# Experts sorted by token count, sixteen small ones taken four at a time in the second half of a mixture-of-experts stage

## The reference

```python
def moe_ffn(x, ...):            # 64 experts, 8 groups of 8, width 256, 8 picks a token
    scores = sigmoid(t @ w_router)
    biased = scores + router_bias
    # best 4 of 8 groups by the sum of their two best, then the best 8 experts in these
    w = scores of the 8 picks / their sum * 2.5
    h = silu(t @ w_gate[e]) * (t @ w_up[e])      # for each expert e
    routed = sum over picked e of w[e] * (h @ w_down[e])
    shared = (silu(t @ ws_gate) * (t @ ws_up)) @ ws_down
    return routed + shared
```

## Time and profile before

| | |
|---|---|
| median of 3 runs | 823.23 us (822.86 to 823.74) |
| profiled execution | 823.12 us |
| its span, first to last instruction | 821.4 us |
| PE busy | 805.8 us (98%) |
| DVE / ACT / POOL busy | 465.0 / 165.9 / 93.2 us |
| moved by DMA | 262.15 MB, mean 319 GB/s |
| gate and up, line 1478 | 1024 matmul records, about 593 ns each |
| granted TensorE clock, mean | 0.997 |

### The profile page before, as it was taken

How to read it: one execution, slowest core, us unless ns; L and a number is a source line. 1 busy time by engine, 2 the same in 40 slices (tenths; PEclk the granted TensorE clock), 3 DMA queues, 4 the chain that set the end, 5 groups by cost and what they waited for, 6 DMA issues and landing times.

```text
span 821.4 us, 11932 instructions
## 1 busy us (share of the span) xinstructions
PE 805.8 (98%) x4283; PEld 501.6 (61%) x4283; DVE 465.0 (57%) x1178; ACT 165.9 (20%) x275; POOL 93.2 (11%) x105
## 2 busy tenths in 40 slices
PE   9999999999999999999999999999999999999995
PEld 7876788888788888544545445454444445445443
DVE  6989899999841357634444334444444434334346
ACT  2210112111221004321211212112121211212126
POOL 1119800000010002100000000000000000000021
PEclk9999999999999999999999999999999999999998
DMA  8433344445489956699999999999999999999991
GB/s 329 157 128 103 117 143 150 155 149 116 141 332 418 412 180 239 215 392 418 423 425 421 423 423 425 421 427 422 422 426 424 422 427 425 421 421 420 419 380 55
DMA packets 45372, 262.15 MB, mean 319 GB/s; under 512 B 9928, under 2 KB 10696, under 8 KB 26256
## 3 DMA queue, kind: packets, MB, share of 16 engines
q1 hardware_dynamic: 40720, 252.88, 77.4%
q0 software_dynamic: 4608, 8.66, 2.8%
HBM read 267.10 MB, written 2.53 MB: 328 GB/s over the span
## 4 chain that ended last, share of the span: by engine, by line
PE 83%; DMA 9%; SPq 5%; ACT 1%; issue 1%; DVE 0%; POOL 0%; ACTq 0%; DVEq 0%; POOLq 0%
PE banks L1269 35%; PE banks L1478 21%; PE banks L1522 10%; PE banks L1441 6%; DMA high<-w_gu 5%; SPq L465 4%; DMA ring<-w_gu 3%; PE banks L1416 3%; SPq L473 2%; PE banks L1284 1%; PE banks L1296 1%; PE banks L1446 1%; PE banks L1495 1%; PE banks L1370 1%; PE banks L1302 1%
## 5 line engine op out<-in xcount | busy, mean ns | idle before, releaser
L1478 PE MATMUL banks<-high,low 128*64 128x512 f32 x848 | 230.1, 593 | 1.1 <-DMA high<-w_gu 1.0
L1269 PE MATMUL banks<-xT,ring 128*128 128x264 f32 x768 | 176.5, 390 | 0.0
L1174 DVE TENSOR_TENSOR cgb<-cgb,banks 128x264 f32<-128x264 f32 x248 | 89.8, 423 | 131.1 <-PE banks L1441 130.9
L1269 PEld LDWEIGHTS banks<-xT,ring 128*128 128x128 f32 x768 | 144.8, 191 | 30.1 <-issue 5.5
L1478 PEld LDWEIGHTS banks<-high,low 128*64 128x64 f32 x848 | 74.0, 137 | 139.4 <-issue 136.4
L1228 DVE SCALAR_TENSOR_TENSOR y_pair<-banks,sml,y_pair 128x1024 fp32r<-128x1024 f32 x31 | 39.8, 1284 | 121.9 <-ACT y_pair L729 121.9
L563 POOL DMA_INDIRECT low<-x_rows_dram,idx x32 | 31.9, 997 | 423.9 <-DVE idx L1118 402.9
L1478 PE MATMUL banks<-ring,low 128*64 128x512 f32 x176 | 77.6, 593 | 1.6 <-DMA ring<-w_gu 1.6
L1441 PEld LDWEIGHTS banks<-sw,y_pair 128*128 128x128 f32 x496 | 63.1, 188 | 25.2 <-issue 24.3
L1522 PE MATMUL banks<-high,mu 128*64 128x512 f32 x336 | 77.2, 599 | 0.0
L1441 PE MATMUL banks<-sw,y_pair 128*128 128x264 f32 x496 | 71.6, 294 | 0.2 <-DVE cgb L1174 0.2
(11 more groups left out here) (300 smaller groups left out, 860.0 us busy)
## 6 DMA issues: line engine op xcount, KB each, us to landing
high<-w_gu SPq DMA_DIRECT2D x35, 2048.0 KB, 24.4
high<-w_dn SPq DMA_DIRECT2D x40, 1024.0 KB, 22.3
ring<-w_front SPq DMA_DIRECT2D x78, 512.0 KB, 3.3
high<-w_gu SPq DMA_DIRECT2D x34, 1024.0 KB, 10.4
ring<-w_gu SPq DMA_DIRECT2D x7, 2048.0 KB, 29.0
us<-w_dn SPq DMA_DIRECT2D x11, 1024.0 KB, 22.4
ring<-w_gu SPq DMA_DIRECT2D x8, 1024.0 KB, 12.2
bgb<-w_dn SPq DMA_DIRECT2D x6, 1024.0 KB, 22.1
```

The source lines that it names most:

```text
L1174: dve.tensor_tensor(acc[:, n], acc[:, n], psum[:, bank, 0:T], ALU.add).then_inc(added, 1)
L1269: ins = pe.matmul(psum[:, 6 + n % 2, 0:T], ring[:, n % RING, k], rhs[:, k], start=(k == 0), stop=(k == KC - 1))
L1478: ins = pe.matmul(psum[SL * j:SL * j + SL, GU_BANK, :], xg[:, k, SL * j:SL * j + SL], gu[slots[j]][:, k], start=(k == 0), stop=(k == KC - 1))
```

## The change

Everything is data that the program finds out while it runs; the weights stay where they are in DRAM.

- **Order.** Experts 0 to 7 keep their places (`FIXED`), since their weights are on the way before the routing is known. The other 56 are ranked by token count: a key per expert (count x 64 + number) is compared with all others on DVE, the ranks become a 0/1 permutation `places`, and PE sorts picks and gates with it inside visit 0: three transposes after k = 1 (`turn_gates`), four matmuls after k = 4 (`sort_gates`), nine small matmuls after the loop (`count_sorted`). The sorted order goes to a table `order`, from which SP reads the expert number of each refill.
- **Quads.** Places 8 to 29 get experts of middling count, two per step as before. From place 30 on a period of eight places holds four of the 16 least used experts, processed in one step with 32 slots each, and then four of the others in two steps of two. The steps become 1 + 12 + 14 + 1 = 28: visit 0, twelve plain ones (six written out, six in a loop that here runs once), fourteen mixed ones written out, with quads at the 3rd, 6th, 9th and 12th, and the last. Overflow (over 32 in a quad, over 64 elsewhere) sets extra turns as before.
- **Buffers.** `dn_7` goes; expert 6's down weights are loaded after visit 0. A quad uses two of the three buffer pairs, and their refills both wait for the quad. Halves are loaded for the pairs of the last two steps but one (`LATE_HALVES = 2`).
- **Rows.** A way to fetch rows by matmul (`gather_rows`, `widen`) is written but not used (`BY_PRODUCTS = 0`): all rows are gathered from DRAM. Two small DMAs load the sample rows for it all the same. The shared expert's down part moves to the quads at steps 3, 6 and 9 of the mixed ones.

The diff, cut to its core:

```diff
+        FIXED = 8
+        MIXED_FROM = 13
+        MIXED = (1, 1, 2) * 4 + (1, 1)
+        STEPS = len(MIXED)
+        BY_PRODUCTS = 0
+        LATE_HALVES = 2
+        QUADS, QUAD_FROM, QUAD_STRIDE = 4, 30, 8
-        LATE_HALVES = 3
+        SHARED_AT = {2: (0, 1, 2), 5: (3, 4, 5), 8: (6, 7)}
...
-        DOWN_PAIRS = ((4, 5), (0, 1), (2, 3), (7, 5), (0, 1), (2, 3))
+        DOWN_PAIRS = ((4, 5), (0, 1), (2, 3))
...
# SP
-                sp.wait_ge(x1_scaled, KC)
-                sp.dma_start(dn[7], w_dn[6]).then_inc(dn_in[7], 16)
...
+                def expert(place):
+                    return sp.value_load(order[0:1, bass.ds(place, 1)] if not isinstance(place, int) else order[0:1, place:place + 1], min_val=0, max_val=E - 1)
+
+                refill(0, 0, SLOT_PAIRS[0], DOWN_PAIRS[0], [6, 7], halves=True)
+                sp.wait_ge(order_ready, 1)
+                for it in range(1, 1 + PER_TURN):
+                    refill(it, it, SLOT_PAIRS[it % 3], DOWN_PAIRS[it % 3], [2 * it + 6, 2 * it + 7], halves=it < EARLY_HALVES, by_place=True)
+                    if it == 1:
+                        sp.wait_ge(weights_ready, 2)
+                        sp.wait_ge(rows_stored, 16 * TC)
+                        for g in range(2):
+                            sp.dma_start(sample_rows[32 * g:32 * g + NS], x_dram[LP:T, HC * P * g:HC * P * (g + 1)]).then_inc(rows_stored, 16)
...
+                for a, pairs in enumerate(mixed_pairs):
+                    for it in pairs:
+                        if it + 3 < PAIRS:
+                            late = PAIRS - 1 - LATE_HALVES <= it + 3 < PAIRS - 1
+                            later_refill(middle, it - PER_TURN, MIXED_FROM - PER_TURN + a, last_refill if it + 3 == PAIRS - 1 else refill, **({"halves": True} if late else {}))
...
# PE, a step: size rows for each of its 2 or 4 experts
+                    slots = [s for r in pairs for s in SLOT_PAIRS[r % 3]]
+                    downs = [s for r in pairs for s in DOWN_PAIRS[r % 3]]
+                    size = 2 * SL // len(slots)
...
+                            ins = pe.matmul(psum[size * j:size * j + size, GU_BANK, :], xg[:, k, size * j:size * j + size], gu[s][:, k],
                                             start=(k == 0), stop=(k == KC - 1))
                         if k == HC - 1:
                             ins.then_inc(gu_mid, 1)
+                        if before is None and k == 1:
+                            turn_gates()
+                        if before is None and k == 4:
+                            sort_gates()
                     ins.then_inc(gu_done, 1)
+                    if before is None:
+                        count_sorted()
```

More of the change, by code:

```diff
@@ L475, in _ @@
-                sp.wait_ge(lists_ready, 1)
[L476 to L487, removed]
@@ new lines, in _, with later_refill @@
+                sp.wait_ge(lists_ready, 1)
+                middle = sp.value_load(rounds[0:1, 1:2], min_val=PLAIN - 1, max_val=MOST - 1)
+                def later_refill(q, it, step, fill, **how):
+                    places = [(q * (2 * PER_TURN) + (2 * it + 6 + j)) % E for j in range(2)]
+                    fill(q * PER_TURN + it, q * PER_TURN + step, SLOT_PAIRS[it % 3], DOWN_PAIRS[it % 3], places, by_place=True, **how)
+                with sp.Fori(0, middle) as q:
+                    for it in range(1 + PER_TURN, 1 + 2 * PER_TURN):
+                        later_refill(q, it, it, refill)
@@ L1179, in sum_last_rows, with visit @@
                     dve.tensor_reduce(dn_sums[:, 1, j:j + 1], dn[DOWN_PAIRS[1][j]][:, 1], AX.X, ALU.add).then_inc(dn_summed[1], 1)
-                def visit(it, u, before=None, last=False):
+                def visit(it, u, before, ahead=None, wide=None, last=False):
                     if last:
@@ L1412, in select, with gather_rows, columns @@
                     ins.then_inc(selected, 1)
+                def gather_rows():
+                    def columns(k):
+                        return psum[:, 2 + k // 4, (k % 4) * P:(k % 4) * P + P]
+                    for k in range(KC):
+                        for c in range(2):
+                            pe.matmul(columns(k), xrow[c][:, k * P:k * P + P], S32[:, c], start=(k % 4 == 0 and c == 0), stop=False)
+                    for h in range(HC):
+                        for g in range(2):
+                            rows = slice(32 * g, 32 * g + NS)
+                            ins = pe.matmul(columns(HC * g + h), sample_rows[rows, h * P:h * P + P], S32[rows, 2], start=False, stop=(h == HC - 1))
+                    ins.then_inc(turned, 1)
@@ new lines, in count_sorted @@
+                def count_sorted():
+                    pe.wait_ge(sort_inputs, SORTED_PICKS)
+                    for c in range(TC + 1):
+                        for b in range(min(c + 1, TC)):
+                            rows = slice(0, tok[b])
+                            before = (tri_spread[rows] if b == 2 else tri16[:]) if b == c else ones16[rows]
+                            ins = pe.matmul(psum[:, SORT_BANKS[0], c * E:c * E + E], before, pk[rows, b], start=(b == 0), stop=(b == min(c, TC - 1)))
+                    ins.then_inc(sort_products, 1)
@@ L1490, in visit @@
                         pe.wait_ge(sw_ready, it)
+                        if isinstance(before, int) and before == 0:
+                            pe.wait_ge(lists_ready, 1)
                         combine(1 - u, before, shared)
@@ L1562, in _, with loads_of @@
-                pairs = pe.snap(turns * PER_TURN + 2)
+                def loads_of(pair):
+                    return 16 * (pair // 3 + 1)
+                visit(0, 0, [0], [16], halves=1, ahead=(4, 2), gathers=16)
+                for k in range(1, 1 + PER_TURN):
+                    visit(k, k % 2, [k], [loads_of(k)], halves=1 + k // 3, before=KC * (k - 1), ahead=(2 * k + 4, 2), gathers=16 * ((k + 1) // 2 + 1))
+                mixed = n_plain(pe)
+                with pe.Fori(1, mixed) as q:
+                    for k in range(1, 1 + PER_TURN):
+                        visit(q * PER_TURN + k, k % 2, [k], [q * 32 + 16 * (k // 3 + 1)], before=q * (PER_TURN * KC) + KC * (k - 1),
+                              ahead=((q * PER_TURN + (k + 2)) % PAIRS * 2, 2), gathers=q * 48 + 16 * ((k + 1) // 2 + 1))
```

437 lines of the change are left out of this document (302 added, 135 removed).

## The result

The kernel after takes 832.01 us (median of five, 831.26 to 833.81) against 823.40 for the kernel before beside it: a ratio of 1.0109, interval 1.0095 to 1.0123, so slower by 8.6 us. Forecast were 826.6 us, slower, in a range of 823 to 832; the direction is right, the size is not: the time lies at the range's very end, 0.01 us beyond it. The profiled execution took 832.09 us, with a span of 830.3 us, 8.9 above that of before.

A forecast was written before the change was run, and what follows sets the result against it. The prediction took the DMA weight stream, full at 423 GB/s, as the bound: 823.12 + 1.2 (stream) + 0.4 (last quad's later start) + 1.8 (cold clock) = 826.5, with 0.1 to the median 826.6 us; range 823 to 832.

The forecast's parts named there:

- What cannot pay: 365 to 781 us: 56 us of PE time saved gains nothing, as the DMA engines have no idle time.
- Rival 3: Whole kernel: PE was the bound after all, so four fewer steps pay, 767 us; chance 0.02.
- Quads and the stream: Mixed steps: a quad takes 14.45 us; queued loads (the cover, 18 us) keep the stream from running dry.
- Quads and the end: Run's end: last quad waits for pair 28's whole gate and up, slack gone, +0.4; cold clock +1.8.
- the cold clock: Last quad: PE idles some 17 us before it and starts at half clock, +1.8 us, bounds 0 and +7.
- Rival 4: Quads run two by two, 24.5 us each, end 10 us later, 836 or more; chance 0.11 with longer cold stretches.
- The sort in visit 0: Visit 0: extra PE work but no wait for DVE, delaying the next loads, +0.7 us together.
- rival 5: Visit 0: DVE's sort chain misses PE by 3 us or more, 830 us; chance 0.07.
- The rows: Before visit 0: shorter queue lets rows be stored sooner and the stream start 0 to 0.7 us earlier, taken as -0.4.
- The moved load: Stream's start: expert 6's down weights, 1.05 MB, now loaded in the stream, +2.5 us, of which 1.5 comes back.
- the thin places: Early stream, rates below 423 GB/s: 330 at 358 to 365 us, closing for -1.5; 270 at 346 to 349.
- More code: Written-out steps fetch more code than loops: doubling the code queue's 0.51 MB would be +1.2 us, taken as +0.2.

The follow-up runs named there:

- e5: Kernel after with pair 28's gate and up weights loaded by halves, so the last quad can start on half a load: 830.25 us.
- e2: Kernel after with throwaway matmuls on PE while it waits for the last quad's third and fourth gate and up buffers: 829.70 us.
- e4: Kernel before with only expert 6's down weights moved, loaded after visit 0 instead of at 323.59: 825.35 us, ratio 1.0020.
- e13: Kernel after without quads, all 18 mixed steps pairs and written out, shared expert's chunks in pairs 25 to 28: 831.24 us.
- e8: Kernel after without quads, 12 of its 18 mixed pair steps back in loops, shared expert's chunks in pairs 25 to 28: 827.74 us.
- e11: Kernel of e9 with 96 increments of an unused semaphore on GpSimd written out behind each of 30 gathers: 834.86 us.
- e9: Kernel before with the loops over turns written out on every engine, nothing else changed: 824.96 us.
- e12: Kernel before, turns still in loops, with 96 increments of an unused semaphore behind every gather of the loop: 838.43 us.
- e1: Kernel after with one line changed, a quad expert's 32 slots taking ranks in the pairs' spread order: 831.43 us, ratio 1.0094.

## Why the prediction was right or wrong

**What cannot pay: right.** Four visits fewer, the same rate of 423 GB/s, PE's time gone into waits. Rival 3 (767) is out.

**Quads and the stream: right.** No slice from 374 us to the last quad falls below 414 GB/s, and the share around the last quad is 1.00 to 1.04; the cover held.

**Quads and the end: right, the size in part by luck.** Forecast +2.2, measured 2.0 (after against e5); from the landing of pair 30's second half to the end 42.5 us, forecast 42 to 43. Its halves are less exact: the cold clock was worth 1.5 us in the quad (2.3 in e2's time, not all of it the clock's), forecast 1.8; whole loads 1.8 (e5), forecast 0.4. The two overlap, presumably as each takes away the same few microseconds ahead of the landing. From the landing at 757.24 to pair 30's gate and up done at 794.01 it is 36.8 us; the sum has 14.45 + 14.04 + 6.87 + 1.8 = 37.2. Rival 4 is out.

**The sort in visit 0: nearly right.** Visit 1's gate and up began at 358.75, 2.9 behind 355.85, of which 0.9 was the start; forecast 1 to 2. PE's extra work was some 2.3 us for 1.8, and its longest wait there 0.34, so rival 5 is out. The rows did come sooner: in an execution 0.8 late the first gather landed at 339.75 (339.63 before), and PE no longer waited for it (0.61 in the earlier trace rows). But PE's own work ahead of it had grown by as much, and its turn began at 340.56 against 339.68, the start's difference: 0 for -0.4.

**The moved load: the step that gave back too much.** I took +2.5 - 1.5 = +1.0; alone it cost 1.9 (e4). The bytes were right; filling the thin places brought 1.1 in the windows and 0.6 in the time.

**More code: the step that failed.** "Steps written out instead of looped fetch more code", doubling it "would be +1.2, I take +0.2": I priced bytes as shared by all lanes, and read one instruction queue of two. Measured, 12 steps written out or looped are 3.5 us (e13, e8), 23 more fetches on q14 alone 8.5 us of landing (e11). At 0.37 us a fetch, an estimate, the kernel after's nine are 3.3 us; how much its three further fetches on q8 add was not measured. By bytes its stream stood 3.6 to 4.1 us behind before's from 370 us on, and pair 30's second half landed 6.6 late, so some 3 us are lateness that the sum over all lanes does not show. Read as a share of 16 lanes q14 is 0.1% of the span; a load waits for the lane that the fetches hold up.

The ledger by spans: before 821.4; moved load 823.8 (e4); sort, table and looped pairs 825.5 (e8), +1.7 with four fetches more; the last quad's landing with pair 28 by halves 828.3 (e5), +2.8 with five fetches more; the quad's end 830.3, +2.0. In the 1.7 and 2.8 the sort's work, the quads' refills and the fetches are not told apart exactly; on q8 e8 has four fetches fewer than before and e5 seven more than e8. Up to 0.8 us of a step is the front's wait, which some executions have and others not. That it is one lane is read from the parts, the 25 GB/s and the packets behind the fetches; the trace does not name the lane of a packet, so whether all of the kernel after's fetches fall on the one that ends last stays open.

So the stream's +1.2, bounds to +4, should have been 6 to 7. The bounds held a sort that is late, which did not happen, and not a lane held up by itself, which did.

## What to carry to other kernels

A stream over many DMA lanes ends with its slowest lane: compare the landings of a load's parts, or the slices where the stream runs dry, before believing a mean share of 1.01. Small traffic that has one lane, such as instruction fetches, is to be priced by that lane; writing out steps, or a loop body grown too long, was paid there. And engine time freed beside a full stream is worth what it can take off the stream: here 11 steps of gathers made by matmuls, with pair 28 by halves, turned a loss of 8.6 us into a gain of 4.6.

## What the runs showed of the hardware that was not expected

- Instruction fetches of 8 KB, 0.32 us each, weighed 0.37 us apiece on a stream bound by DMA (e11 over e9), some eighteen times their share of sixteen lanes (0.32 / 16 = 0.02 us), and 0.57 in e12 over before.
- A fetch also slowed the packet behind it: 0.66 us for 8 KB instead of 0.31, in e12_padded_loops.
- A loop was no shelter by itself: with 576 instructions more in its body, GpSimd's loop led to as many fetches as the same code written out (41 each, 13 without).
- Even gathers did not help a stream that another lane held up: with the fifteen quicker parts 3 us closer together (e1) the time moved by 0.6.
